# A decoder trunk on one core: output projections by token tile, all four of their weight blocks split ahead, and a new slotting of the row multiply-adds

## What is computed

```
mod = einsum("bd,lde->lbe", silu(c), ada_w) + ada_b          # 6 rows of 1024 per layer
for l in range(2):
    sh1, sc1, g1, sh2, sc2, g2 = split(mod[l])
    u = x * (1 + sc1) + sh1
    if l == 0:  y = short_conv_mixer(u)      # (u @ w_in), gate, 3-tap convolution, gate, @ conv_w_out
    else:       y = nsa_mixer(u, ...)        # attention (compressed, selected, window), @ w_o
    x = layer_norm(ALPHA * x + g1 * y, ln_g[l, 0], ln_b[l, 0])
    u = x * (1 + sc2) + sh2
    y = grouped_moe(u, router_w, router_bias, w_gu[l], w_down[l])
    x = layer_norm(ALPHA * x + g2 * y, ln_g[l, 1], ln_b[l, 1])
```

## Time and profile before

| | us |
|---|---|
| median of 3 runs | 1482.23 (1479.53 to 1485.29) |
| profiled execution, its own time | 1481.74 |
| profiled execution, span | 1479.9 |
| TensorE busy | 1292.0 (87%) |
| DVE busy | 1081.8 (73%) |
| ACT busy | 770.4 (52%) |
| POOL busy | 301.6 (20%) |

### The profile page before, as it was taken

One profiled execution on the slowest core, in us unless ns is written; L12 is line 12 of the kernel. 1 busy time (PEld: TensorE's weight loads), 2 busy tenths in 40 slices (PEclk: granted clock), 3 DMA queues, 4 the chain that ended last, 5 costly groups with the idle time before them and its releaser, 6 DMA issues.

```text
span 1479.9 us, 18395 instructions
## 1 busy us (share of the span) xinstructions
PE 1292.0 (87%) x6603; PEld 1003.2 (68%) x6603; DVE 1081.8 (73%) x1201; ACT 770.4 (52%) x998; POOL 301.6 (20%) x344
## 2 busy tenths in 40 slices
PE   1399997849999999987989899999984999999985
PEld 0277765747777777746987677775783777777762
DVE  5648783768889888855884676665368898889867
ACT  0323221317777777754443555567142777777760
POOL 3011111410000000016101554545251100000020
PEclk9699998859999999997989899999976999999998
DMA  8657775319999999951711333330633999999972
GB/s 307 233 178 242 268 245 211 137 48 356 411 389 380 387 390 378 399 198 43 219 62 58 101 101 92 106 117 4 242 114 115 375 403 389 387 384 385 397 286 86
DMA packets 107568, 356.07 MB, mean 241 GB/s; under 512 B 8034, under 2 KB 16446, under 8 KB 107470
## 3 DMA queue, kind: packets, MB, share of 16 engines
q1 hardware_dynamic: 82984, 269.52, 48.6%
q0 software_dynamic: 19952, 69.83, 13.5%
q10 hardware_dynamic: 4566, 15.84, 2.6%
HBM read 330.99 MB, written 25.21 MB: 241 GB/s over the span
## 4 chain that ended last, share of the span: by engine, by line
PE 39%; issue 30%; DVE 15%; ACT 7%; DMA 5%; POOL 3%; ACTq 0%; DVEq 0%; POOLq 0%
PE bank L233 9%; PE bank L235 8%; PE bank L234 8%; DVE acc L361 3%; PE bank L1927 2%; PE bank L1909 2%; DMA xg<-scratch_u,tok 2%; POOL prob L2144 2%; ACT w_hi L1107 2%; PE bank L1897 1%; DMA ada<-in_ada_w_dram 1%; PE bank L894 1%; DVE xt L594 1%; ACT prob L2045 1%; POOL xg L1043 1%
## 5 line engine op out<-in xcount | busy, mean ns | idle before, releaser
L1113 DVE TENSOR_TENSOR w_lo<-raw,w_hi 128x2048 fp32r<-128x2048 f32 x189 | 436.9, 2316 | 69.5 <-ACT w_hi L1107 67.5
L1107 ACT ACTIVATE w_hi<-raw 128x2048 fp32r<-128x2048 f32 x189 | 362.5, 1919 | 84.9 <-PE bank L235 75.0
L233 PE MATMUL bank<-w_lo,xe_hi 128*128 128x512 f32 x512 | 211.9, 414 | 9.6 <-DVE xe_lo L1070 9.4
L235 PE MATMUL bank<-w_hi,xe_hi 128*128 128x512 f32 x512 | 203.8, 398 | 0.0
L234 PE MATMUL bank<-w_hi,xe_lo 128*128 128x512 f32 x512 | 203.6, 398 | 0.0
L228 DVE TENSOR_TENSOR w_lo<-raw,w_hi 128x2048 fp32r<-128x2048 f32 x37 | 85.5, 2316 | 114.2 <-ACT w_hi L223 114.0
L233 PE MATMUL bank<-u_lo,w_hi 128*128 128x512 f32 x320 | 133.7, 418 | 17.8 <-DVE q L1814 9.3
L1043 POOL DMA_INDIRECT xg<-scratch_u,tok x32 | 36.2, 1132 | 554.3 <-DVE tok L1037 553.7
L223 ACT ACTIVATE w_hi<-raw 128x2048 fp32r<-128x2048 f32 x37 | 70.5, 1910 | 139.0 <-PE bank L235 137.3
L234 PE MATMUL bank<-u_hi,w_lo 128*128 128x512 f32 x320 | 129.8, 406 | 0.0
L235 PE MATMUL bank<-u_hi,w_hi 128*128 128x512 f32 x320 | 129.8, 406 | 0.0
(11 more groups left out here) (289 smaller groups left out, 2357.6 us busy)
## 6 DMA issues: line engine op xcount, KB each, us to landing
raw<-in_w_gu_dram SPq DMA_DIRECT2D x128, 1024.0 KB, 7.7
raw<-in_w_down_dram SPq DMA_DIRECT2D x64, 1024.0 KB, 8.3
ada<-in_ada_w_dram POOLq DMA_DIRECT2D x64, 512.0 KB, 5.4
ada<-in_ada_w_dram SPq DMA_DIRECT2D x32, 512.0 KB, 3.8
scratch_y<-ye ACTq DMA_DIRECT2D x30, 512.0 KB, 7.5
raw<-in_conv_w_in_dram SPq DMA_DIRECT2D x12, 1024.0 KB, 11.8
raw<-in_w_kv_dram SPq DMA_DIRECT2D x6, 1024.0 KB, 8.5
rows<-scratch_mods POOLq DMA_DIRECT2D x10, 512.0 KB, 7.4
```

The source lines that it names most:

```text
L233: nc.tensor.matmul(o, lh, rl, start=start, stop=False)
L235: return nc.tensor.matmul(o, lh, rh, start=False, stop=stop)
L1107: nc.scalar.activation(w_hi[:, hslot, :], raw[:, slot, :], ACT.Copy).then_inc(hi_done, 1)
L1113: nc.vector.tensor_tensor(w_lo[:, slot, :], raw[:, slot, :], w_hi[:, hslot, :].bitcast(F32), ALU.subtract).then_inc(lo_done, 1)
```

## The change

It has four parts.

1. The row multiply-adds get a table, `MACS`, with up to six to a slot and none in the last two, and the sums stand ahead of blocks 2, 3, 5, 8, 9 and 11 (`SUM_AT`).
2. The output projections of both layers go by token tile: a unit (`proj_unit`, 12 products) is one tile, one n, one kh. Two tiles use banks 0, 1 and two 2, 7, then the same again, so tile i waits for the residual of tile i-2. The fourth weight block is split into a buffer of its own (`w_hi4`, `split_hi_last`, `split_lo_last`), in layer 1 in attention step 42.
3. `proj_tail_pe` puts the turns and routers of tiles 0 to 2 between the units of tiles 2 and 3. DVE and ACT do a tile's residual, statistics, coefficients and norm behind each tile (`front_dve`, `front_act`); the router's and token rows are made behind tile 1; the scale row goes to `us` and no longer takes a row slot; the gate row is loaded first.
4. Around it: some low splits and the `x_rows_dve` operations change places, the stores of `us` stand between the weight loads on SP, and the gather's window has one split.

```diff
+        w_hi4 = at("w_hi4", [P, BLK], F32R, U0)
...
+        def split_hi_last(act, b):
+            act.wait_ge(raw_in[b % NRAW], 16 * (b // NRAW + 1))
+            act.wait_ge(blk_used, b - 3)
+            nc.scalar.activation(w_hi4[:], raw[:, b % NRAW, :], ACT.Copy).then_inc(hi_done, 1)
...
-                if n >= 4:
-                    pe.wait_ge(*s.hi.at(n - 3))
+                if n >= 2:
+                    pe.wait_ge(*s.hi.at(n - 1))
...
+        PROJ_BANKS, LOGIT_BANK, COLS_BANK = ((0, 1), (2, 7), (0, 1), (2, 7)), 3, 4
...
+        def proj_unit(pe, s, v, i, n, kh, ready=None):
+
+            b = s.b0 + 2 * n + kh
+            if i == 0:
+                pe.wait_ge(lo_done, b + 1)
+            if i >= 2 and kh == 0:
+                pe.wait_ge(*s.res.at(2 * (i - 2) + n + 1))
...
+        def proj_tail_pe(pe, s, v, moe):
+
+            proj_unit(pe, s, v, 2, 0, 0)
+            cols_pe(pe, moe)
+            proj_unit(pe, s, v, 2, 0, 1)
+            turn_pe_plain(pe, moe.turn, xt[:, 0, :], 0)
+            proj_unit(pe, s, v, 2, 1, 0)
+            turn_pe_plain(pe, moe.turn, xt[:, 1, :], 1)
+            proj_unit(pe, s, v, 2, 1, 1)
+            router_pe(pe, moe, 0)
+            proj_unit(pe, s, v, 3, 0, 0)
+            router_pe(pe, moe, 1)
+            proj_unit(pe, s, v, 3, 0, 1)
+            proj_unit(pe, s, v, 3, 1, 0)
+            turn_pe_plain(pe, moe.turn, xt[:, 2, :], 2)
+            proj_unit(pe, s, v, 3, 1, 1)
+            router_pe(pe, moe, 2)
...
-        MACS_FIRST, MACS_SLOT = 16, 4
+        MACS_FIRST = 16
+        MACS = (6, 6, 6, 2, 6, 4, 6, 6, 5, 1, 0, 0)
+        SUM_AT = {2: 2, 3: 3, 5: 4, 8: 5, 9: 6, 11: 7}
...
-                if b >= 3 and b % 2 == 1:
-                    mod_sums(pe, ada_a, (b + 1) // 2, bank[4:6])
+                if b in SUM_AT:
+                    mod_sums(pe, ada_a, SUM_AT[b], bank[4:6])
...
-            mod_sums(pe, ada_a, 7, bank[4:6])
...
+            pe.wait_ge(conv_v, 4 + 1)
+            proj_unit(pe, cout, v, 0, 0, 0)
+            pe.wait_ge(conv_v, 4 + 2)
+            proj_unit(pe, cout, v, 0, 1, 0)
+            pe.wait_ge(conv_lo, 2 * 4)
+            pe.wait_ge(*ada_a.row_made.at(2 * (ada_a.j1 - ada_a.j0)))
+            proj_unit(pe, cout, v, 0, 0, 1)
+            proj_unit(pe, cout, v, 0, 1, 1)
...
                 split_hi(act, b + NSPLIT)
-                if b >= 3 and b % 2 == 1:
-                    mod_rows(act, ada_a, (b + 1) // 2, bank[4:6])
-                    mod_store(act, ada_a, (b + 1) // 2)
-            mod_rows(act, ada_a, 7, bank[4:6])
-            mod_store(act, ada_a, 7)
+                if b in SUM_AT:
+                    mod_rows(act, ada_a, SUM_AT[b], bank[4:6])
+                    mod_store(act, ada_a, SUM_AT[b])
...
                 split_lo(dve, b + NSPLIT)
-                ada_macs(dve, ada_a, MACS_FIRST + MACS_SLOT * b, MACS_SLOT)
+                ada_macs(dve, ada_a, MACS_FIRST + sum(MACS[:b]), MACS[b])
...
         def front_act(act, s, b0):
...
             for i in range(TT):
                 norm_root(act, s.ln0, i)
                 norm_apply(act, s.ln0, i)
+                if i == TT - 2:
+                    split_hi(act, b0 + 4)
+                turn_act(act, s.turn, u_t, i)
+                if i == TT - 2:
+                    split_hi(act, b0 + 5)
+            split_hi(act, b0 + 6)
...
+        def front_dve(dve, s, proj, b0, times):
+            ln = s.ln0
             dve.wait_ge(x_back, 16 * TT * times)
...
             for i in range(TT):
+                if i == TT - 1:
+                    split_lo(dve, b0 + 4)
+                    x_rows_dve(dve, s, 0)
+                for n in range(2):
+                    proj_residual(dve, proj, ln, n, i)
+                    dve.wait_ge(*proj.res.at(2 * i + n + 1))
+                    norm_stats_half(dve, ln, i, n)
                 if i == TT - 1:
                     row_free(dve, ln.gate)
+                norm_stats_end(dve, ln, i)
+                norm_coef(dve, ln, i)
+                if i == 1:
+                    router_rows_dve(dve, s)
+                    token_rows_dve(dve, s)
+            split_lo(dve, b0 + 5)
...
-        O_STEPS = (36, 38, 40)
+        O_STEPS = (36, 38, 40, 42)
```

More of the change, by code:

```diff
@@ L486, in __init__, with norm_stats_half, norm_stats_end @@
                     Count("ln_" + n, TT) for n in ("stat", "root", "coef", "norm", "gain", "done"))
[L488 to L493, removed]
+        def norm_stats_half(dve, s, i, h):
+            nc.vector.bn_stats(ln_stat[:, i, 6 * h:6 * h + 6], xt[:, i, h * BANK:(h + 1) * BANK]).then_inc(dve_step, 1)
+            dve_n[0] += 1
+        def norm_stats_end(dve, s, i):
             dve.wait_ge(dve_step, dve_n[0])
@@ L496, in norm_stats @@
                               ).then_inc(s.stat.sem, 1)
+        def norm_stats(dve, s, i):
+            for h in range(2):
+                norm_stats_half(dve, s, i, h)
+            norm_stats_end(dve, s, i)
         def norm_root(act, s, i):
@@ L556, in __init__ @@
                 self.b0, self.mm, self.res = b0, Count("proj_mm", 2 * (TT - 1)), Count("proj_gated", 2 * TT)
[L558 to L579, removed]
@@ new lines, in proj_unit @@
+        def proj_unit(pe, s, v, i, n, kh, ready=None):
[4 more added lines that the diff above has]
+                pe.wait_ge(*s.res.at(2 * (i - 2) + n + 1))
+            w_h = w_hi4[:] if n == 1 and kh == 1 else w_hi[:, b % NSPLIT, :]
+            wh = w_h.rearrange("p (k n) -> p k n", k=4)
+            wl = w_lo[:, b % NRAW, :].rearrange("p (k n) -> p k n", k=4)
+            t = slice(i * P, (i + 1) * P)
+            for kk in range(4):
+                k = 4 * kh + kk
+                if ready is not None:
+                    pe.wait_ge(ready, k + 1)
+                vh, vl = v(k)
+                m = mm3(bank[PROJ_BANKS[i][n]][:], vh[:, t], vl[:, t], wh[:, kk, :], wl[:, kk, :],
+                        start=(k == 0), stop=(k == KD - 1))
+            if i == TT - 1:
+                m.then_inc(blk_used, 1)
+            elif kh == 1:
+                m.then_inc(s.mm.sem, 1)
@@ L898, in cols_pe, with front_pe @@
         def cols_pe(pe, s):
-            pe.wait_ge(*s.pre_in.at(16 * 9))
-            nc.tensor.transpose(bank[s.proj_banks[7]][:, 0:6 * KD], mod_r[:], ident[0:6 * KD, 0:6 * KD]
+            pe.wait_ge(*s.pre_in.at(16 * 10))
+            nc.tensor.transpose(bank[COLS_BANK][:, 0:6 * KD], mod_r[:], ident[0:6 * KD, 0:6 * KD]
                                 ).then_inc(s.logit.sem, 1)
-        def front_pe(pe, s, proj):
-            pe.wait_ge(*proj.res.at(TT))
-            turn_pe_plain(pe, s.turn, xt[:, 0, :], 0)
-            router_pe(pe, s, proj, 0)
-            for i in range(1, TT):
-                turn_pe_plain(pe, s.turn, xt[:, i, :], i)
-                router_pe(pe, s, proj, i)
+        def front_pe(pe, s):
+            turn_pe_plain(pe, s.turn, xt[:, TT - 1, :], TT - 1)
+            router_pe(pe, s, TT - 1)
         def route_dve(dve, s):
@@ L1368, in moe_sp @@
             load_part(sp, s, 0, 0, -1, w_gu, 0, 1)
+            u_store(sp, s, 0)
             load_part(sp, s, 0, 0, 0, w_gu, 0, 2)
             load_part(sp, s, 0, 0, 1, w_gu, 0, 3)
+            u_store(sp, s, 1)
             load_part(sp, s, 0, 0, 2, w_gu, 1, 0)
             load_part(sp, s, 0, 0, 3, w_gu, 1, 1)
-            for i in range(TT):
-                sp.wait_ge(*s.u_made.at(2 * i + 2))
-                sp.dma_start(s.u[i * P:(i + 1) * P, :], us[:, i % 2, :]).then_inc(s.u_out[i % 2].sem, 16)
+            u_store(sp, s, 2)
+            u_store(sp, s, 3)
             step_load(sp, s, 0, 0, first=4)
@@ L2025, in attention_pe @@
             values_pe(pe, units_of(NS - 2))
-            out_tile_pe(pe, 0, 0, 1)
+            proj_unit(pe, wo, v_parts, 1, 0, 0)
             values_pe(pe, units_of(NS - 1))
-            out_tile_pe(pe, 0, 0, 2)
-            out_tile_pe(pe, 0, 0, 3)
-            for n, kh in ((0, 1), (1, 0), (1, 1)):
-                for i in range(TT):
-                    out_tile_pe(pe, n, kh, i)
+            proj_unit(pe, wo, v_parts, 0, 1, 0)
+            pe.wait_ge(*ada_b2.row_made.at(8))
+            proj_unit(pe, wo, v_parts, 1, 1, 0)
+            proj_unit(pe, wo, v_parts, 0, 0, 1, ready=att_olo)
+            proj_unit(pe, wo, v_parts, 0, 1, 1)
+            proj_unit(pe, wo, v_parts, 1, 0, 1)
+            pe.wait_ge(att_tc, NU)
+            proj_unit(pe, wo, v_parts, 1, 1, 1)
+            proj_tail_pe(pe, wo, v_parts, moes[1])
         def exp_act(act, u):
```

157 lines of the change are left out of this document (60 added, 97 removed).

## The result

The changed kernel takes 1523.76 us (median of 4 runs, 1521.08 to 1525.14), the kernel before 1481.89 beside it (4 runs, 1479.53 to 1485.29): a ratio of 1.0272, interval 1.0257 to 1.0288, so 42 us slower where 18 were forecast.

What follows compares the result with a forecast made beforehand. TensorE's in-order queue, busy 87% of the span, was taken to set the end; 39.4 - 16.0 - 2.3 + 1.0 - 3.9 + 1.0 - 1.0 = +18.2 on 1481.7 gave 1500 us, range 1486 to 1510.

Steps and rivals of the forecast that it cites:

- Part 1: Convolution stage: row sums one block behind their slot make TensorE wait 31.3 us; stage +39.4 us (bounds 32 and 42).
- The clock term: Convolution stage: TensorE's slow restarts after four pauses, 1.8 us each, 7.2 us together (bounds 0 and 10).
- Part 2: Behind the convolution: the 12.4 us wait and the slow 3.6 us sum go, -16.0 us.
- Part 3: Layer 0's tail, projection to route: -2.3 us, 2.7 lost behind the first unit included; POOL's +1.0 counted besides.
- Part 5: Around each layer's first expert: second part's low split comes earlier, -0.5 a layer, -1.0 us (bounds 0 and -2).
- keeps its chain: Route to first expert product, 21.7 us, was to stay unchanged, the moved split fitting into the gather's wait.
- POOL in Parts 3 and 4: Both layers' tails: POOL's scaling of tile 2 stretches DVE's work ahead of tile 3, 0 to 2.0, taken as +1.0 per layer.
- TensorE's own walk: Layer 0's tail: TensorE's units, turns and routers counted from T, the convolution's end, router 2 done at T+58.2.
- The sum worked out beside it in the prediction: By the skill page's exclusion of DVE and GpSimd, each layer pays 2.0 us for POOL, the sum 2 us more.
- The faster one: Rival: row sums don't hold TensorE, multiply-adds being done when the block before ends; 1461 us, chance 0.08.
- The one that washes out: Rival: waits cost 31.3 but restarts nothing, POOL doesn't collide, DVE doesn't hold tile 3; +4.4, 1486 us, chance 0.12.
- The late parameter rows: Rival: in layer 0 parameter rows land at T+37 (T: convolution's end), the transpose waits 9 us; 1508 us, chance 0.12.

Runs made afterwards that it cites:

- E1: Changed kernel, six multiply-adds to a slot kept, row sums two blocks behind their slot, ACT's row copy ahead of the high split: 1492.36 us.
- E5: Kernel before with only the changed kernel's table of multiply-adds and places of the row sums: 1515.67 us.
- E2: Changed kernel with the first expert's low splits put back behind DVE's row operations and places: 1510.26 us.
- E10: E7's kernel, block 16's low split behind tile 3's coefficients, the expert's third-block low split behind the row operations of tiles 0 and 1: 1459.34 us.
- E9: Changed kernel with one wait more: POOL's scaling of tile 2 waits until tile 3's statistics are taken: 1522.06 us.
- E7: E4's kernel with five and four multiply-adds to a slot, sums moved to match, the last between the first two projection units: 1465.82 us.
- E4: Changed kernel with E1's and E2's edits, and tile 0's row operations moved from ahead of tile 3's residual into the gather's wait: 1472.87 us.

## Why the prediction was right or wrong

**Right, Part 1 (+39.4, measured +40.3).** Pauses of 8.26, 9.74, 10.25 and 3.10 us were forecast as 7.6, 10.0, 10.6 and 3.1, with their releasers; E1 and E5 show the cause from both sides. The first is 0.7 too long: block 1 ended 1.1 us later than I had it, and a multiply-add of DVE at 98.33 waited 1.75 us for its load. The clock term was right in its sum by luck and wrong in its parts. What is left of 40.3 after the pauses (31.35), the sum moved in (1.8) and the old waits (-0.95) is 8.1, against 7.2 for four restarts. Of it 1.1 lies ahead of the first pause (the later end of block 1); the other 7.0 belong to three restarts, some 2.3 each, and none to the fourth. The windows of TensorE after (length, busy, clock, DMA share, GB/s):
```profile
104.40:108.00 3.60, 3.54 (x5) 0.50 0.93 348
130.10:133.80 3.70, 3.62 (x5) 0.50 0.94 293
166.70:170.40 3.70, 3.62 (x5) 0.50 0.95 281
221.00:228.00 7.00, 6.94 (x26) 1.00 0.97 363
```

**Right, Part 2 (-16.0, measured -16.0)**, and the 2.7 behind the first unit in Part 3 (2.86). E5 shows that it needed the new order of units too.

**Wrong, the failed step: Part 5, "the second part's low split comes earlier, at most 0.9 us were waited there: -0.5 a layer".** Measured +6.0 and +7.2, of which 4.7 a layer is TensorE's longer pause and the rest the slow restart behind it. I counted what stood behind the wait and not what stood ahead of it: the moved low splits wait for a high split whose buffer TensorE frees only while it works through the first expert. What the step itself asked, to name what is queued behind the waiting instruction, I did not do here, though I did it for TensorE in Part 1. Tile 3's row operations and the places, 6.5 us, which filled the wait before, came behind it. In the table this step is off by 14.2 of the 21.2 us by which the span was off, and E2 took 13.5 back.

**Wrong in the same part: route to first product "keeps its chain".** It grew by 0.9 and 0.8 us: DVE's low split of 2.28 us now starts with POOL's gather issue, which lasted 1.06 longer. The split is as much longer than the row operation that had stood there (1.22). E10 took it back.

**Mis-sized, POOL in Parts 3 and 4 (1.0 a layer).** It is 3.2 us: 0.98 on the low split, 2.17 on the row operation. In layer 0 TensorE's own walk was right: its last work ahead of the pause ended at T+58.3, forecast T+58.2; the last turn came at T+66.3 instead of T+63.5 with POOL's 1.0 in it, and the tail at +1.5 instead of -1.3. Layer 1 gave 1.1 instead of 2.9. The bound of 2.0 came from one stretched row of DVE (0.69 us took 2.73) and was about right for one operation: the row operation was stretched by 2.17, the small one in E9 by 2.16. But two operations stand ahead of tile 3, and both met POOL. The rows read as if the engines took turns: POOL's first operation ends at 311.63 and DVE's low split at 313.78, POOL's second at 316.01 and the row operation at 317.09, each about its own 1.1 to 2.3 us behind the one before. So what a stretch costs is what is left of the other engine's operation, not a share of one's own. The Trainium skill's page "SBUF — State Buffer", section "SBUF: two separate sides", has the two exclude each other; these rows agree. The sum worked out beside it in the prediction, 2.0 a layer, would have been nearer and still 1.2 short.

**The rivals.** The faster one's condition, all multiply-adds done when the block before ends, did not hold; made to hold (E7) with the other two repairs it gave its kind of time, 1466. The one that washes out had all three conditions against it: restarts did cost, POOL did collide, and DVE did hold tile 3. The late parameter rows did not come: no pause for them in layer 0. My bounds for Part 5 (0 and -2) allowed no loss in it at all, and the result lies 14 us above the range's end, about the size of this one step.

## What to carry to other kernels

Where an instruction is moved ahead of others on an in-order engine, ask first when its own input exists; if that hangs on a buffer that the consumer has yet to free, everything that it was moved past is moved behind the consumer. Where, as here, a slot's work starts only when its block is done, a sum that needs it should stand two blocks behind the slot, not one, and a slot's work should be spread evenly, or its loads come late. Taking two engines apart in time pays only if the work, once moved, meets nothing else that the path needs.

## What the runs showed of the hardware

**A slow restart is not a function of the pause's length alone.** After 3.10 us without work (before 221.06) TensorE's window reads 1.00, full clock; after 2.86 us (before 264.38) it reads 0.61, half the clock at first:
```profile
264.30:268.00 3.70, 3.62 (x10) 0.61 0.48 158
```
In E1, with the same pause of 2.86 us at the same place, the clock stays at 1.00 from 233 to 240 us; in E4 the first two products behind it take 0.47 and 0.44 us and the next seven 0.63, so the first product alone doesn't tell. Behind the last turn of h, with the same pauses of 2.32 and 1.41 us, the changed kernel starts at full clock (first product 0.50) and falls to half a few products later; E9 is at half clock from the start (0.80) and again behind its next pause of 1.96, where the changed kernel, after 1.39, is not. From that first product to the last root passed 39.0 and 41.5 us. What else the granted clock hung on in these cases stays open. It is worth some 2 us an event, and a difference of that size can't be read from one profile of each. The Trainium skill's page "TensorE: Matmul & The Clock Gate", section "Part 1: The HAM clock gate", has the clock follow the array's recent activity; no run here tells which part of it decided.

**POOL and DVE stretch each other.** A POOL operation on 128x1024 takes 2.35 us alone and 4.30 beside DVE's low split; DVE's go from 2.28 to 3.27 and from 1.22 to 3.39, and one of 0.22 us to 2.38 (E9). The issue of an indirect gather on POOL goes from 1.84 to 2.90 where DVE's operation is 1.06 longer: it ends 0.9 us behind the end of the DVE operation that started just before it, in the kernel before (318.46 and 317.54), in the changed one (345.28 and 344.35) and in E10 (302.71 and 301.79).
